# A 2,048-wide fp32 block on one Trainium2 core: recurrence and mLSTM in portions beside the third input product

## What is computed

```python
p = h @ w_in[l]
(lru_x, lru_z, ml_u, ml_o, ml_z, ml_i, ml_f,
 mo_q, mo_k, mo_v, mo_z) = jnp.split(p, SPLIT_POINTS, axis=-1)
y_lru = rg_lru_branch(lru_x, lru_z, ...)      # 512 wide: conv of 4 taps, gates, linear recurrence, SiLU gate
y_ml = mlstm_branch(ml_u, ml_o, ml_z, ml_i, ml_f, ...)   # 768 wide: 4 heads, 2 chunks of 128 tokens
y_mo = moba_branch(mo_q, mo_k, mo_v, mo_z)    # 768 wide: 6 heads of causal attention with a linear bias
y = jnp.concatenate([y_lru, y_ml, y_mo], axis=-1)
x = x + y @ w_out[l]
```

## Time and profile before

| | |
|---|---|
| runs, us | 2064.4, 2070.97, 2070.53 (median 2070.53) |
| profiled execution, us | 2065.26 (span 2063.5) |
| mean granted PE clock | 0.927 of full |
| PE busy | 1826.5 us, 89% |
| DVE busy | 1437.9 us, 70% |
| ACT busy | 810.0 us, 39% |
| read from HBM | 307.23 MB, 150 GB/s over the span |

### The profile page before, as it was taken

How to read it: one execution, slowest core, us unless ns; L and a number is a source line. 1 busy time by engine, 2 the same in 40 slices (tenths; PEclk the granted TensorE clock), 3 DMA queues, 4 the chain that set the end, 5 groups by cost and what they waited for, 6 DMA issues and landing times. The chain is left out here.

```text
span 2063.5 us, 26961 instructions
## 1 busy us (share of the span) xinstructions
PE 1826.5 (89%) x10559; PEld 1552.1 (75%) x10559; DVE 1437.9 (70%) x2250; ACT 810.0 (39%) x1269; POOL 7.2 (0%) x18
## 2 busy tenths in 40 slices
PE   7999914689969987899999998999689999999797
PEld 6999903479949976688888787887687877676597
DVE  5888575488867766788778777866873477776444
ACT  6544333044344543523333223322553454443343
POOL 1000000000000000000000000000000000000000
PEclk9999955589979998899999999999799999999898
DMA  6688600068727633334545553754242454332352
GB/s 214 210 264 268 203 2 3 1 198 266 246 91 252 199 106 120 119 120 140 168 158 194 177 199 123 227 171 143 92 134 76 146 169 134 122 118 86 99 183 94
DMA packets 168991, 311.10 MB, mean 151 GB/s; under 512 B 14904, under 2 KB 23452, under 8 KB 168864
## 3 DMA queue, kind: packets, MB, share of 16 engines
q1 hardware_dynamic: 162176, 305.70, 45.7%
q10 hardware_dynamic: 6240, 3.62, 0.6%
q0 software_dynamic: 448, 0.06, 0.0%
HBM read 307.23 MB, written 2.10 MB: 150 GB/s over the span
## 5 line engine op out<-in xcount | busy, mean ns | idle before, releaser
L480 PE MATMUL bank<-operand,w_high 128*128 128x256 f32 (+1 forms) x2720 | 869.2, 320 | 37.1 <-DVE operand L634 13.3
L481 PE MATMUL bank<-operand,w_high 128*128 128x256 f32 (+1 forms) x2720 | 860.2, 316 | 0.0
L482 PE MATMUL bank<-operand,w_low 128*128 128x256 f32 (+1 forms) x2720 | 859.6, 316 | 0.0
L298 DVE TENSOR_TENSOR w_low<-raw,w_high 128x1024 fp32r<-128x1024 f32 (+4 forms) x416 | 457.1, 1129 | 221.3 <-ACT w_high L288 220.3
L480 PEld LDWEIGHTS bank<-operand,w_high 128*128 128x128 f32 x2720 | 524.5, 193 | 95.4 <-issue 28.2
L288 ACT ACTIVATE w_high<-raw 128x1024 fp32r<-128x1024 f32 (+4 forms) x416 | 397.0, 981 | 495.6 <-PE bank L482 356.2
L482 PEld LDWEIGHTS bank<-operand,w_low 128*128 128x128 f32 x2720 | 524.3, 193 | 31.3
L481 PEld LDWEIGHTS bank<-operand,w_high 128*128 128x128 f32 x2720 | 524.6, 193 | 30.8
L413 DVE SCALAR_TENSOR_TENSOR ada_acc<-ada_raw,silu_c,ada_acc 128x512 f32<-128x512 f32 x720 | 490.6, 747 | 6.5 <-DMA ada_raw<-in_ada_w 4.3
L480 PE MATMUL bank<-operand_small,w_high 128*128 128x512 f32 (+1 forms) x320 | 125.2, 391 | 11.6 <-DVE big L396 5.4
L481 PE MATMUL bank<-operand_small,w_high 128*128 128x512 f32 (+1 forms) x320 | 121.1, 379 | 0.0
(11 more groups left out here) (341 smaller groups left out, 1415.5 us busy)
## 6 DMA issues: line engine op xcount, KB each, us to landing
ada_raw<-in_ada_w SPq DMA_DIRECT2D x192, 512.0 KB, 4.0
raw<-in_w_in SPq DMA_DIRECT2D x96, 512.0 KB, 4.9
raw<-in_pool_w_in SPq DMA_DIRECT2D x64, 512.0 KB, 5.2
raw<-in_mla_w_in SPq DMA_DIRECT2D x48, 512.0 KB, 4.4
raw<-in_w_out SPq DMA_DIRECT2D x32, 512.0 KB, 5.3
raw<-in_pool_w_out SPq DMA_DIRECT2D x32, 512.0 KB, 5.7
raw<-in_mla_w_out SPq DMA_DIRECT2D x32, 512.0 KB, 4.6
raw<-in_xa_wkv SPq DMA_DIRECT2D x16, 512.0 KB, 4.7
```

Source lines behind the costliest of these rows:

```text
L298: ins = nc.vector.tensor_sub(view(LO[:, slot, ks, :], False), view(RAW[:, slot, ks, :], True), view(HI[:, slot, ks, :], False).bitcast(F32))
L480: pe.matmul(out_, hi, x[:, 0, :], start=first, stop=False, skip_group_check=True)
L481: pe.matmul(out_, hi, x[:, 1, :], start=False, stop=False, skip_group_check=True)
L482: return pe.matmul(out_, lo, x[:, 0, :], start=False, stop=last, skip_group_check=True)
```

## The change

The stages `lru` to `win_c` become one stage, `middle`. It loops over the 24 chunks of `win_c`; after each chunk c PE runs `pe_beside(pe, c)`, ACT after its conversion `act_beside(act, c)`, DVE `dve_beside(dve, c)`: the same operations of the five stages, cut into portions. On DVE the units of the chunk follow the portion. Eight units leave `win_c` (16 stay) and go to `mixo` (20 instead of 12, two with each of four chunks in its first two groups). The first chunk of `win_c` is converted at the end of `front`. As `win_c` writes its 24 tiles while the branches still read theirs, its results lie elsewhere (`MIXED`), and temporaries lie in the half of the operand buffers that is not yet used (`spare`, `SMALL`). `win_c` keeps to banks 0 to 3, the portions to 5, 6 and 7. Small DMAs (gate weights, masks) are issued by ACT between `win_a` and `win_b`. The stage ends between the old stages are gone. Pairs of units of the mLSTM share a portion, so some waits now name the second of a pair.

```diff
--- before.py
+++ after.py
@@ buffers and products @@
-UC, QT, KT = 16, 22, 67
-VT, KTOK, EX, SOT = 40, 73, 28, 48
+KT, KTOK = 67, 73
+MIXED = [16 + n for n in range(16)] + [67, 68, 69, 70, 48, 49, 50, 51]
+MQ, MK, MV, MZ = MIXED[0:6], MIXED[6:12], MIXED[12:18], MIXED[18:24]
-    win_c = Product("win_c", w_in, 4, 6, 4, 1, "copy1", dest=MQ, col0=3336)
+    win_c = Product("win_c", w_in, 4, 6, 4, 1, "copy1", dest=MIXED, col0=3336, banks=4)
@@ units of the modulation weights per chunk @@
-    ada = {win_a: 1, win_c: 1, xo: 1, po: 2}
+    ada = {win_a: 1, xo: 1, po: 2}
-              mixo: {(i, j): 1 for i in range(4) for j in (1, 2, 3)}}
+              win_c: {divmod(c, 4): n for c, n in ((2, 1), (3, 1), (7, 1), (8, 1), (9, 1), (10, 2), (11, 1), (12, 1), (15, 1),
+                                                   (19, 1), (21, 2), (22, 2), (23, 1))},
+              mixo: {(i, j): 2 if i < 2 and j >= 2 else 1 for i in range(4) for j in range(4)}}
@@ scratch over the operand's unused half @@
+        XSF = nc.alloc_sbuf_tensor_at("scratch", [P, KD, 2, 2 * T], F32, offset=XS_AT)
+        PSF = nc.alloc_sbuf_tensor_at("scratch_small", [P, KC, 2, 2 * T], F32, offset=PS_AT)
@@ act_front, dve_front: first chunk converted there @@
-        PRIMED = {"mfinish": [win_c], "moba": [mixo], "cross": [xo], "pairs": [mo]}
+        PRIMED = {"front": [win_c], "moba": [mixo], "cross": [xo], "pairs": [mo]}
             act_product(act, win_b, former=win_a)
+            act_high(act, win_c, 0, 0)
             dve_product(dve, win_b)
+            dve_low(dve, win_c, 0, 0)
@@ the portions @@
+        def pe_beside(pe, c):
+            if c == 1:
+                pe.wait_ge(lw_in, 32)
+                pe_lru(pe, 0)
+                pe_lru(pe, 1)
+            elif c == 2:
+                pe_lru(pe, 2)
+                pe_lru(pe, 3)
+                pe_out_gate(pe, 0)
+                pe_out_gate(pe, 1)
+            elif c == 3:
+                for i in range(2, 6):
+                    pe_out_gate(pe, i)
+            elif 5 <= c <= 10:
+                pe_project(pe, c - 5)
+            elif c == 11:
+                pe_mgates(pe)
+            elif c == 12:
+                for h in range(3):
+                    pe_states(pe, h)
+            elif c == 13:
+                pe_states(pe, 3)
+                pe_scores(pe, 0)
+                pe_scores(pe, 1)
+            elif 14 <= c <= 17:
+                u = 2 * (c - 14)
+                pe_values(pe, u)
+                pe_values(pe, u + 1)
+                if u < 6:
+                    pe_scores(pe, u + 2)
+                    pe_scores(pe, u + 3)
+            elif c == 19:
+                for i in range(6):
+                    pe_finish(pe, i)
+
+        def act_beside(act, c):
+            s = nc.scalar.activation
+            if c == 0:
+                act.dma_start(rF, BIG[4:8, G, :]).then_inc(fg_in, 16)
+                lru_act.inc(s(sp4, V["lru_lambda"], ACT.Abs), "abs")
+                lru_act.inc(s(sp4, sp4, ACT.Exp, scale=-1.0), "exp")
+                for i in range(3):
+                    act_out_gate(act, i)
+            elif c == 1:
+                for i in range(3, 6):
+                    act_out_gate(act, i)
+                mg_dve.wait(act, "f")
+                mg_act.inc(s(rY, rF, ACT.Abs), "abs")
+                mg_act.inc(s(rY, rY, ACT.Exp, scale=-1.0), "exp")
+            elif c in (2, 3):
+                act_lru_gates(act, 2 * c - 4)
+                act_lru_gates(act, 2 * c - 3)
+            elif c == 4:
+                for i in range(5):
+                    act_silu(act, i)
+            elif c == 5:
+                act_silu(act, 5)
+            elif 6 <= c <= 11:
+                act_projected(act, c - 6)
+                if c == 8:
+                    for i in range(6):
+                        mf_act.inc(s(tile(O + i), tile(Z + i), ACT.Sigmoid), "z", i)
+                if c == 10:
+                    act_rates(act)
+                if c == 11:
+                    act_lru_decay(act)
+            elif c == 13:
+                for h in range(4):
+                    act_weights(act, h)
+                for h in range(3):
+                    act_states(act, h)
+            elif c == 14:
+                act_states(act, 3)
+            elif c == 15:
+                for b in range(4):
+                    lru_dve.wait(act, "q2", b)
+                    lru_act.inc(s(lq(b), lq(b), ACT.Sqrt), "sq", b)
+            elif 16 <= c <= 19:
+                act_spread(act, 2 * c - 32)
+                act_spread(act, 2 * c - 31)
+            elif c == 22:
+                lru_dve.wait(act, "y", 3)
+                for i in range(6):
+                    mf_dve.wait(act, "y", i)
+                    act_split(act, "ml", i, tile(Z + i), XS[:, 4 + i, 0, T:2 * T])
+                act.dma_start(DIST, a["dist"].rearrange("(q p) k -> p q k", p=P)).then_inc(dist_in, 16)
+            elif c == 23:
+                for b in range(4):
+                    act_split(act, "lru", b, tile(LX + b), XS[:, b, 0, T:2 * T])
+
+        def dve_beside(dve, c):
+            if c == 0:
+                dve_gate_bias(dve)
+                dve_lru_conv(dve, 0)
+                dve_lru_conv(dve, 1)
+            elif c == 1:
+                dve_lru_conv(dve, 2)
+                dve_lru_conv(dve, 3)
+                dve_ml_conv(dve, 0)
+            elif c == 2:
+                dve_ml_conv(dve, 1)
+                dve_ml_conv(dve, 2)
+            elif c == 3:
+                dve_ml_conv(dve, 3)
+                dve_ml_conv(dve, 4)
+                dve_out_gate(dve, 0)
+                dve_out_gate(dve, 1)
+            elif c == 4:
+                dve_ml_conv(dve, 5)
+                dve_lru_scale(dve)
+                for i in range(2, 6):
+                    dve_out_gate(dve, i)
+            elif c == 5:
+                for i in range(6):
+                    dve_silu(dve, i)
+                for n in range(9):
+                    dve_blocks(dve, n)
+            elif c == 6:
+                for n in range(9, 18):
+                    dve_blocks(dve, n)
+                dve_lru_gates(dve, 0)
+                dve_lru_gates(dve, 1)
+            elif c == 7:
+                mg_act.wait(dve, "exp")
+                dve_log1p(dve, mg_dve, rY, rT, rZ, rZ2, rZ)
+            elif c == 8:
+                dve_forget(dve)
+            elif c == 9:
+                dve_maxima(dve)
+            elif c == 10:
+                dve_lru_gates(dve, 2)
+                dve_lru_gates(dve, 3)
+            elif c == 11:
+                for i in range(6):
+                    mf_act.wait(dve, "z", i)
+                    mf_dve.inc(nc.vector.tensor_tensor(tile(Z + i), tile(Z + i), tile(O + i), ALU.mult), "z", i)
+            elif c == 12:
+                dve_weights(dve)
+                for h in range(4):
+                    dve_keys(dve, h)
+            elif c == 13:
+                dve_lru_root(dve, 0)
+                dve_lru_root(dve, 1)
+            elif c == 14:
+                dve_probs(dve, 0)
+                dve_probs(dve, 1)
+                dve_lru_root(dve, 2)
+                dve_lru_root(dve, 3)
+            elif 15 <= c <= 18:
+                u = 2 * (c - 15)
+                if u < 6:
+                    dve_probs(dve, u + 2)
+                    dve_probs(dve, u + 3)
+                dve_values(dve, u)
+                dve_values(dve, u + 1)
+                if u:
+                    dve_head_norm(dve, u - 2)
+                    dve_head_norm(dve, u - 1)
+            elif c == 19:
+                dve_head_norm(dve, 6)
+                dve_head_norm(dve, 7)
+                dve_lru_scan(dve, 0)
+                dve_lru_scan(dve, 1)
+            elif c == 20:
+                dve_lru_scan(dve, 2)
+                for i in range(6):
+                    dve_finish(dve, i)
+            elif c == 21:
+                dve_lru_scan(dve, 3)
+            elif c == 23:
+                for i in range(6):
+                    dve_split(dve, "ml", i, tile(Z + i), XS[:, 4 + i, 1, T:2 * T], XS[:, 4 + i, 0, T:2 * T])
+                for b in range(4):
+                    dve_split(dve, "lru", b, tile(LX + b), XS[:, b, 1, T:2 * T], XS[:, b, 0, T:2 * T])
+
+        def pe_middle(pe):
+            for c in range(24):
+                i, j = divmod(c, 4)
+                pe_chunk(pe, win_c, i, j, slab_after(win_c, i, j))
+                pe_beside(pe, c)
+
+        def act_middle(act):
+            for c in range(24):
+                i, j = divmod(c, 4)
+                if c:
+                    act_high(act, win_c, i, j)
+                if j == 0 and i:
+                    act_evac(act, win_c, i - 1)
+                act_beside(act, c)
+            act_evac(act, win_c, 5)
+
+        def dve_middle(dve):
+            for c in range(24):
+                i, j = divmod(c, 4)
+                if c:
+                    dve_low(dve, win_c, i, j)
+                dve_beside(dve, c)
```

(15 more changed lines are left out.)

604 lines of the change are left out of this document (286 added, 318 removed).

## The result

The changed kernel takes 1982.76 us (median of 4 runs, 1981.49 to 1984.55), the kernel before 2068.45 on the same chip: ratio 0.9588, 95% interval 0.9568 to 0.9608. Forecast was 1985; the kernel before had its median at 2070.5 then, so -4.1% was forecast and -4.1% came. The profiled execution took 1982.54, span 1980.7 (before 2063.5: -82.8).

A forecast was written before the change was run, and what follows sets the result against it. PE was taken to bound the whole program, DVE the new stage `middle` (212 against 183 us). The profiled 2065.3 less 90.6 in `middle`, plus 7 in `mixo` and 3 to the median, gave 1985 us, range 1970 to 2010.

The forecast's parts named there:

- The sum for the middle: Stage `middle`: DVE's list of 212.4 us plus 10.5 of waits ends at 482.4 instead of 573.0, -90.6 us.
- chunk 12: In `middle`, DVE waits for PE's row maxima, which stand behind chunk 11; 2 us.
- Distance: In `middle`, a whole chunk between result and reader keeps DVE's waits at 10.5 us, near the lower bound.
- ACT's nine DMA issues: Between `win_a` and `win_b`, some 4 us in ACT's queue, hidden under conversions done a chunk ahead; cost 0.
- `mixo`, +7: Eight more units in `mixo`: second group +2.9, late loads in the first +2, slab +2; bounds 0 and 21.2.
- The 2.9 for a second group: In `mixo`'s second group, DVE's list with six units is 29.4 us against the group's 26.5.
- The clock: In `middle`, half clock for about 5 us behind PE's waits at chunks 4, 7, 18, 21, about 2.3 us each.
- 1 (waits come back): In `middle`, 40% of the small stages' waits return and late conversions cost as much again; +20, 2005 us; chance 0.17.
- 2: In `middle`, every chunk begins at half clock, making PE's list 238 against DVE's 223; +15, 2000 us; chance 0.10.
- 4: PE stays at half clock through the whole of `middle`; +22, 2087 us; chance 0.02.
- 5: Little gain: time goes to `mixo` and later stages, all 21.2 us of units exposed; 2020 us; chance 0.05.
- 3 (better hidden): DVE waits only for the DMA in `middle` (-8) and `mixo` hides the units (-7); 1970 us; chance 0.08.

The follow-up runs named there:

- e2: Changed kernel with the 16 modulation units in `middle` working on 64 of their 512 columns (result incomplete); 1969.55 us.
- e5: Changed kernel with PE's matmuls of the portions (projections, states, scores, values) issued twice; 2003.92 us.
- e10: Changed kernel with three units moved to chunks 14, 16 and 17, and units in chunks 14 to 17 ahead of DVE's portion; 1981.62 us.
- e6: Changed kernel with DVE's portions from 13 on one chunk earlier, removing the chunk between result and reader; 2045.72 us.
- e9: Changed kernel with the 20 units in `mixo` working on 64 of their 512 columns (result incomplete); 1980.99 us.
- e8: Changed kernel with four units moved to `win_b`, convolutions before gates' bias, first chunk converted before `win_b`'s copies, and a small Sigmoid in chunk 21; 1962.00 us.
- e3: Changed kernel with units placed as in the kernel before, 24 in the middle and 12 in `mixo`; 1994.79 us.
- e1: Changed kernel with DVE's first two convolutions ahead of adding the gates' bias to the forget rows in chunk 0; 1980.04 us.
- e4: Changed kernel with four of the middle's 16 units done in `win_b` instead; 1972.61 us.
- e7: Changed kernel with ACT converting the middle's first chunk ahead of its copies out of `win_b`; 1978.27 us.
- e11: e8 with five units in `win_b` and eleven in the middle, those of chunks 14 to 17 ahead of the portion, none from 18 on; 1972.48 us.

## Why the prediction was right, and where it was not

**The sum for the middle.** -90.6 was forecast, -92.1 came. Start to end of DVE's work is 261.1 to 482.9, 221.8 us; less the 11.2 of waits it is 210.6, forecast 212.4. The waits, forecast and measured: the DMA 2.1 and 4.1 (it is issued only at 261.2, behind the conversion of the first chunk), chunk 12 2 and 0.3, the scores 3.5 and 3.0, the slab 2 and 2.1, conversions 0.9 and 1.7. PE waits 32 us, forecast about 40, and its list was too short: 183 forecast, 191.8 busy.

**What in it was luck.** I took the longer of two totals. `e2` and `e5` show that this rule holds for neither engine at the margin: 28.6 us off DVE's list gave 13.1, 26.0 us on PE's cost 17.9. The sum came out, as I read it, because in this kernel PE's list is the longer one only in the third piece, and by little: there PE is full for 44.2 us while DVE is busy for 40.39, and most of that difference stood in my waits for scores and slab as a guess. A sum chunk by chunk would have had a place for this; I did not make one for the whole stage, and the layout that I judged in that way, `e10`, missed too.

The total owes something to luck as well. The 3 us that I added from the profiled execution to the median did not come (1982.54 and 1982.76), the 2.2 at the start that nobody forecast did, and 3.5 more in `moba` stood against 3.5 less in `mixo`.

**Distance** was the argument for 10.5 instead of 50 us of waits; `e6` shows it, at twice my price.

**ACT's nine DMA issues** cost nothing, as said: they stood in ACT's queue from 228.6 to 234.4, 5.8 us and not 4, the two conversions behind them came 3.0 and 0.9 us late against `win_a`'s first matmul, and the product from `win_a`'s first matmul on took the same time as before to within 0.1 us.

**`mixo`, +7.** This term was mis-sized: +3.5. The slab's 2 fit (2.0 left in `e9`). The 2.9 for a second group in which DVE's list is longer than 26.5, and the 2 for loads behind late units, came to at most 1.5 together. I counted what is over a group's 26.5 us as lost; that the groups behind have room for it, as DVE converts ahead of PE, is how I read the rest, and no run shows it apart.

**`moba`, 0.** Not in the working at all: +3.5. 1.3 are the table: the last functions that ACT ran before `moba` used to leave the Sigmoid's table, now it is a Sqrt's, and PE's transposes wait for ACT behind the load. `e8` shows it by taking it away. The Trainium skill, "ScalarE: Activation LUTs", section "What ACT_TABLE_LOAD costs", has the load at some 1283 ns, and a drain of some 1380 ns with it, at every switch to another set. The trace agrees on the load with its 1.28; of the drain nothing shows at this place, where PE's first wait changed by 1.28 (3.72 and 2.44). I had not asked what the last function before the stage would be. The other 2 are PE at half clock in the last head, where its last three groups of matmuls took 1.12, 2.08 and 3.63 us instead of 0.66, 1.25 and 3.44. `e3` agrees: its `moba` has the table's load and, like the kernel before, 27.3 us at half clock (37.5 in the changed kernel), and took 51.0.

**The clock.** In the changed kernel's stage PE fell to 0.50 for 3.4 to 6.8 us after its waits of 2.9 to 5.0 us, behind DVE's portions 0, 3, 4, 7 and 18, and after the gap at the stage's start; after waits of 1.9 and less it did not. I had named 4, 7, 18 and 21: three of these, and behind 21 the wait was 1.9. The case of the Trainium skill cited in the prediction has a wait ahead of every burst of matmuls; that every chunk would begin at half clock did not come true in this stage (mean 0.95), and PE's list of waits has 12 for DVE's conversions over 24 chunks.

The other traces show that this is no fixed border. In `e1` the clock also fell at three waits of 1.9. And in `e2`, `e3`, `e4`, `e6`, `e7`, `e9` and `e10` it fell right behind chunk 11's portion, 14 matmuls of 4 rows in 2.4 us, with no wait of PE there. Windows of `e4`, where PE had no wait over 0.25 us since 339.7:

```profile
366.50:370.00 3.50, 3.50 (x25) 2.86 (x24) 3.50 (x5) 3.50 (x7) 0.00 (x0) 1.00 0.08 29
370.00:373.40 3.40, 3.40 (x17) 3.39 (x17) 3.23 (x10) 3.24 (x8) 0.00 (x0) 0.50 0.81 257
```

`e9` has the changed kernel's code up to there; its clock fell, and the changed kernel's did not.

Behind portions 0, 3, 4 and 18 PE waited for DVE again further on by as much as half clock had cost it, so I take it that the stage lost nothing there. Behind 7 it may have: PE ran at 0.50 up to 344.3 and then had no wait until 409.8, while DVE waited 4.4 us for conversions, maxima and scores. At half clock from 339.0 to 344.3 PE does 2.6 us less of its list. No run shows that part by itself.

**Rivals.** 1 (waits come back) would have shown as more than 11.2 of DVE's waits, 2 and 4 as a clock under 0.75, 5 as a `mixo` 21 longer: none did. 3 (better hidden: 8 off the waits, 7 off `mixo`) was wrong for the waits and half right for `mixo`.

## What to carry to other kernels

When two engines run lists of work side by side, compare them chunk by chunk, not in total; the total can be right and still tell nothing of what the next us is worth. Put a whole chunk between a result and its reader. Before filling an engine's idle time, see whether the list of waits has a name for it: pauses between chained operations are not filled by work put ahead of the chain. And look at a stage's borders on their own: what ACT's last function was, which slab closes there, what stands ahead of the first conversion.

## What the runs showed of the hardware

TensorE's granted clock can fall to 0.50 with PE busy all the time: in seven of the twelve profiles after the change it did so within 1.2 us of the end of 14 matmuls of 4 rows that stood among the product's dense ones (above), and in five it did not.

`moba` is the same program in all of these kernels but for line numbers (and `e8`'s and `e11`'s table), yet it took 50.7 to 54.0 us in the twelve profiles after the change, with 27 to 41 us of it at half clock. PE works there in bursts of 0.7 to 2 us with waits of 0.7 to 4.5 between them. The length doesn't follow the share at half clock alone (`e3` 51.0 with 27.3, the changed kernel 52.9 and `e8` 50.7 with 37.5, `e9` 54.0 with 41.0). That it matters on which head the slow stretch falls is my reading; no run shows it apart. A few us at such a stage are not to be read as an effect of an edit elsewhere.
